# Opening the second block in one stage: norms and turning of both inputs, taps and both stores together

## The reference, cut to what matters

```python
mod_x = adaln(c, ada_w[i], ada_b[i])
mod_c = adaln(c_ctx[None], ada_w[i], ada_b[i])
h_c = modulate(ctx, norm1_g[i], mod_c[0], mod_c[1])     # rms norm, gain, scale and shift
h_x = modulate(x, norm1_g[i], mod_x[0], mod_x[1])
qkv_c, z_c, al_c, be_c, cq_c, ckv_c, kr_c, gt_c = jnp.split(h_c @ w_in[i], IN_OFFSETS, axis=-1)
qkv_x, z_x, al_x, be_x, cq_x, ckv_x, kr_x, gt_x = jnp.split(h_x @ w_in[i], IN_OFFSETS, axis=-1)
# qkv then goes through a depthwise convolution of 5 taps (conv_w) and SiLU
...
x_mid = x + mod_x[2] * mix_x                            # x itself is needed again much later
```

## Time and profile before

| | us |
|---|---|
| median of 3 runs | 3594.99 |
| lowest, highest | 3583.04, 3594.99 |
| profiled execution, its time | 3596.75 |
| profiled execution, its span | 3595.0 |
| TensorE busy (matmul) | 3052.2 (85%) |
| VectorE, ScalarE, GpSimd busy | 1256.0, 644.9, 250.3 |
| mean granted TensorE clock | 0.915 |

### The profile page before, as it was taken

The page is one execution under the profiler, slowest core; times in us unless marked ns, Lnnn a source line. Parts: engine busy times, 40 slices in busy tenths (PEclk is TensorE's granted clock), DMA queues, the critical chain, the costliest instruction groups (busy, mean ns, idle before and its releaser), DMA issues. The chain is left out here.

```text
span 3595.0 us, 44471 instructions
## 1 busy us (share of the span) xinstructions
PE 3052.2 (85%) x18941; PEld 1813.9 (50%) x18941; DVE 1256.0 (35%) x2385; ACT 644.9 (18%) x1413; POOL 250.3 (7%) x347
## 2 busy tenths in 40 slices
PE   5899398899896689997999978897977678888888
PEld 2343374346574355556888863365433343333343
DVE  1001753176343159714556545642001221111111
ACT  2000331101332135302112111431010100000000
POOL 0000010000000000003334310100000000000000
PEclk8999579898897889998999989999988879999999
DMA  9321001322001311100000012102112339999998
GB/s 313 134 70 68 0 1 38 87 72 72 1 1 46 140 36 47 34 19 9 2 2 3 2 51 87 41 1 94 70 70 82 145 134 413 413 413 413 413 413 352
DMA packets 161245, 431.74 MB, mean 120 GB/s; under 512 B 33006, under 2 KB 44530, under 8 KB 159893
## 3 DMA queue, kind: packets, MB, share of 16 engines
q1 hardware_dynamic: 161050, 428.90, 31.7%
HBM read 418.22 MB, written 10.66 MB: 119 GB/s over the span
## 5 line engine op out<-in xcount | busy, mean ns | idle before, releaser
L306 PE MATMUL banks<-weight_ring,rows_turned 128*128 128x512 f32 (+1 forms) x680 | 282.1, 575 | 33.6 <-DMA weight_ring<-in_w_in 29.5
L242 PE MATMUL banks<-weight_ring,branch_turned 128*128 128x512 f32 x640 | 280.9, 600 | 33.2 <-DMA weight_ring<-in_w_in 18.5
L2091 PE MATMUL banks<-rows_turned,weight_ring 128*128 128x256 f32 (+1 forms) x768 | 252.9, 489 | 0.8 <-PEq L431 0.5
L3140 PE MATMUL banks<-expert_weights_early,chosen_turned 128*64 128x512 f32 (+1 forms) x864 | 210.5, 563 | 20.1 <-DMA expert_weights_early<-in_w_up 15.4
L242 PE MATMUL banks<-weight_ring,rows_turned 128*128 128x512 f32 x512 | 221.6, 593 | 3.0 <-PE banks L242 1.9
L306 PEld LDWEIGHTS banks<-weight_ring,rows_turned 128*128 128x128 f32 x680 | 127.0, 197 | 186.9 <-issue 185.5
L242 PEld LDWEIGHTS banks<-weight_ring,branch_turned 128*128 128x128 f32 x640 | 122.2, 192 | 189.4 <-issue 170.7
L2091 PEld LDWEIGHTS banks<-rows_turned,weight_ring 128*128 128x128 f32 x768 | 147.2, 192 | 99.8 <-issue 84.9
L3140 PE MATMUL banks<-weight_ring,chosen_turned 128*64 128x512 f32 (+1 forms) x672 | 173.2, 570 | 13.1 <-DMA weight_ring<-in_w_up 10.5
L242 PEld LDWEIGHTS banks<-weight_ring,rows_turned 128*128 128x128 f32 x512 | 96.6, 190 | 128.0 <-issue 128.0
L242 PE MATMUL banks<-weight_ring,mix_turned 128*128 128x512 f32 x320 | 140.7, 601 | 8.4 <-DMA weight_ring<-in_l_w_out 7.1
(11 more groups left out here) (544 smaller groups left out, 4485.7 us busy)
## 6 DMA issues: line engine op xcount, KB each, us to landing
expert_weights_early<-in_w_gate SPq DMA_DIRECT2D x36, 1408.0 KB, 19.4
expert_weights_early<-in_w_up SPq DMA_DIRECT2D x36, 1408.0 KB, 16.8
expert_weights_early<-in_w_down SPq DMA_DIRECT2D x44, 1024.0 KB, 18.5
weight_ring<-in_w_gate SPq DMA_DIRECT2D x28, 1408.0 KB, 19.7
weight_ring<-in_w_up SPq DMA_DIRECT2D x28, 1408.0 KB, 17.9
weight_ring<-in_w_down SPq DMA_DIRECT2D x36, 1024.0 KB, 17.6
weight_ring<-in_l_w_in SPq DMA_DIRECT2D x15, 2048.0 KB, 8.5
weight_ring<-in_w_in SPq DMA_DIRECT2D x13, 2048.0 KB, 9.0
```

Source lines behind the costliest of these rows:

```text
L242: ins = nc.tensor.matmul(kit.ps[0:m, u % 8, 0:cols], lhsT, rhs, start=(k0 + j == 0), stop=(k0 + j == matrix.nk - 1))
L306: ins = kit.nc.tensor.matmul(kit.ps[0:m, u % self.banks, 0:cols], lhsT, rhs, start=(k == 0), stop=(k == nk - 1))
L2091: ins = nc.tensor.matmul(kit.ps[:, bank(u), 0:n], w[:, k, f * P:(f + 1) * P], hT[:, k, h0:h0 + n], start=(k == 0), stop=(k == KD - 1))
L3140: ins = nc.tensor.matmul(kit.ps[64 * s:64 * s + 64, 3 * mat + i, 0:nn], xe[:, p % 2, k0 + j, s * CAP:(s + 1) * CAP], w[s][:, j, n0:n0 + nn ...
```

## The change

The opening of the second block becomes one stage, `second_opening`, ahead of `project_and_convolve`:

- SP issues, one behind the other, the loads of the norm-1 gain, the context, the taps and the constants, then the store of x; it waits until all four tiles of x have been taken, issues the store of `h_park`, and waits for taps and constants. Both stores are waited for only in the projection's stage, behind its weight loads.
- The context has a place of its own: with the squares, the scaled rows (three rooms in place of two) and the taps it lies in `qk`, a tensor that is only written from the projection on.
- ScalarE squares x's four tiles, takes their root, takes row 0's group out of PSUM, squares the context's two tiles (waiting for their load), takes their root, and takes the groups of rows 1 to 5.
- VectorE waits for the gain first and joins it with the modulation; the rest is the order of before, over six tiles, with a second reciprocal ahead of tile 4.
- TensorE turns six tiles, then the taps (waiting for taps and constants); VectorE and ScalarE copy the taps after their last rows.
- The norm-2 gain isn't loaded here any more.

```diff
-        load(kit, [(const[:, :], a["constants2"]), (g12[:, 0, :], as_columns(a["norm1_g_2"][0])), (g12[:, 1, :], as_columns(a["norm2_g_2"][0]))])
...
-                norm_and_turn(kit, x, list(range(TX)), hT[:, :, CTX:], gx[:, 0, :], cols[:, 0:8, 0])
-                store(kit, [(x_park, x[:, :, :]), (h_park, hT[:, :, CTX:])])
-                load(kit, [(x[:, 0:TC, :], a["ctx_2"][0].rearrange("(t p) d -> p t d", p=P))])
-                norm_and_turn(kit, x, list(range(TC)), hT[:, :, 0:CTX], gx[:, 1, :], cols[:, 0:8, 1])
...
+                cwT = kit.sb(hs, "conv_w_turned", [P, 3 * HEADS, 5])
+                parked = second_opening(kit, stream, a, x, const, hT, cwT, gx, g12, cols, qk, (x_park, h_park))
+                project_and_convolve(kit, stream, m["in_first"], hT, qk, raw_v, small, cwT, parked)
...
+def second_opening(kit, stream, a, x, const, hT, cwT, gx, g12, cols, scratch, parks):
...
+        def sync(sp):
+            with nc.allow_non_contiguous_dma("columns of small vectors"):
+                sp.dma_start(g12[:, 0, :], as_columns(a["norm1_g_2"][0])).then_inc(gain_landed.sem, 16)
+                sp.dma_start(ctx[:, :, :], a["ctx_2"][0].rearrange("(t p) d -> p t d", p=P)).then_inc(ctx_landed.sem, 16)
+                sp.dma_start(cw, a["conv_w_2"][0]).then_inc(loaded.sem, 16)
+                sp.dma_start(const[:, :], a["constants2"]).then_inc(loaded.sem, 16)
+            sp.dma_start(x_park, x[:, :, :]).then_inc(parked.sem, 16)
+            for side in range(2):
+                sp.wait_ge(taken[side].sem, taken[side](TX))
+            sp.dma_start(h_park, hT[:, :, CTX:]).then_inc(parked.sem, 16)
+            sp.wait_ge(loaded.sem, loaded(32))
...
+        def scalar(act):
+            def square(i):
+                if i:
+                    act.wait_ge(sums.sem, sums(i))
+                if i == TX:
+                    act.wait_ge(ctx_landed.sem, ctx_landed(16))
+                nc.scalar.activation(sq, rows[i][0], ACT.Square, scale=D ** -0.5, accum_out=ss[:, i:i + 1]).then_inc(sums.sem, 1)
+            for i in range(TX):
+                square(i)
+            act.wait_ge(sums.sem, sums(TX))
+            root(kit, ss[:, 0:TX]).then_inc(rooted.sem, 1)
+            take(act, 1, 0)
+            for i in range(TX, R):
+                square(i)
+            act.wait_ge(sums.sem, sums(R))
+            root(kit, ss[:, TX:]).then_inc(rooted.sem, 1)
+            for i in range(1, R):
+                take(act, 1, i)
+            for g in range(1, NT // 4, 2):
+                take_taps(act, 1, g)
+
+        def vector(dve):
+            dve.wait_ge(gain_landed.sem, gain_landed(16))
+            for i in range(2):
+                ins = nc.vector.scalar_tensor_tensor(gx[:, i, :], cols[:, 8:16, i], 1.0, g12[:, 0, :], ALU.add, ALU.mult)
+            ins.then_inc(gains_ready.sem, 1)
+
+            def scale(i):
+                if i in (0, TX):
+                    end = TX if i == 0 else R
+                    dve.wait_ge(rooted.sem, rooted(1 + (i > 0)))
+                    step(dve, nc.vector.reciprocal(ss[:, i:end], ss[:, i:end]))
+                if i >= 3:
+                    dve.wait_ge(turned.sem, turned(2 * (i - 2)))
+                nc.vector.tensor_scalar(xs[:, i % 3, :], rows[i][0], ss[:, i:i + 1], None, ALU.mult).then_inc(scaled.sem, 1)
+            scale(0)
+            for i in range(R):
+                if i + 1 < R:
+                    scale(i + 1)
+                take(dve, 0, i)
+            for g in range(0, NT // 4, 2):
+                take_taps(dve, 0, g)
+
+        def tensor(pe):
...
+            for i in range(R):
+                pe.wait_ge(scaled.sem, scaled(i + 1))
...
+            pe.wait_ge(loaded.sem, loaded(32))
+            for i in range(NT // 4):
+                g = 2 * R + i
+                free(g)
+                for n in range(4):
+                    ins = nc.tensor.transpose(kit.ps[:, g % 8, 5 * n:5 * n + 5], cw[:, (4 * i + n) * P:(4 * i + n + 1) * P], kit.ident[0:5, 0:5])
+                ins.then_inc(turned.sem, 1)
...
-        load(kit, [(cw, a["conv_w_2"][0])])
-        turn(kit, [([cw[:, f * P:(f + 1) * P] for f in range(f0, f0 + 4)], cwT[:, f0:f0 + 4, :]) for f0 in range(0, NT, 4)])
...
         def sync(sp):
             stream.load_ahead(sp, matrix.last + 1, 0)
+            sp.wait_ge(parked.sem, parked(32))
```

More of the change, by code:

```diff
@@ L2004, in second_block @@
                 hT = kit.sb(hs, "rows_turned", [P, KD, CTX + SEQ])
-                norm_and_turn(kit, x, list(range(TX)), hT[:, :, CTX:], gx[:, 0, :], cols[:, 0:8, 0])
-                store(kit, [(x_park, x[:, :, :]), (h_park, hT[:, :, CTX:])])
-                load(kit, [(x[:, 0:TC, :], a["ctx_2"][0].rearrange("(t p) d -> p t d", p=P))])
-                norm_and_turn(kit, x, list(range(TC)), hT[:, :, 0:CTX], gx[:, 1, :], cols[:, 0:8, 1])
-                project_and_convolve(kit, stream, m["in_first"], a, hT, qk, raw_v, small)
+                cwT = kit.sb(hs, "conv_w_turned", [P, 3 * HEADS, 5])
+                parked = second_opening(kit, stream, a, x, const, hT, cwT, gx, g12, cols, qk, (x_park, h_park))
+                project_and_convolve(kit, stream, m["in_first"], hT, qk, raw_v, small, cwT, parked)
                 elementwise(kit, vector=lambda dve: step(dve, nc.vector.tensor_copy(ab[:, :, :], small[:, :, 0:32])))
@@ L2022, in second_block, with take, take_taps, free @@
         second_half(kit, stream, m, a, x, out, place3, (x_park, h_park, s_park, y_park, rows_park), cols)
-def project_and_convolve(kit, stream, matrix, a, hT, qk, raw_v, small):
+def second_opening(kit, stream, a, x, const, hT, cwT, gx, g12, cols, scratch, parks):
+    nc = kit.nc
+    step = kit.dve_step
+    R = TX + TC
+    NT = 3 * HEADS
+    flat = scratch[:, :, :].rearrange("p c n -> p (c n)")
+    ctx = flat[:, 0:TC * D].rearrange("p (t d) -> p t d", d=D)
+    sq = flat[:, TC * D:(TC + 1) * D]
+    xs = flat[:, (TC + 1) * D:(TC + 4) * D].rearrange("p (i d) -> p i d", d=D)
+    cw = flat[0:5, (TC + 4) * D:(TC + 4) * D + DN_QKV]
+    x_park, h_park = parks
+    parked = kit.counter("parked", 32)
+    with ExitStack() as st:
+        ss = kit.sb(st, "square_sums", [P, R])
+        rows = [(x[:, t, :], CTX + t * P, gx[:, 0, :], cols[:, 0:8, 0]) for t in range(TX)]
+        rows += [(ctx[:, t, :], t * P, gx[:, 1, :], cols[:, 0:8, 1]) for t in range(TC)]
+        gain_landed = kit.counter("gain_landed", 16)
+        ctx_landed = kit.counter("rows_landed", 16)
+        loaded = kit.counter("loaded", 32)
+        sums = kit.counter("row_sums", R)
+        rooted = kit.counter("roots_ready", 2)
+        scaled = kit.counter("rows_scaled", R)
+        turned = kit.counter("turned", 2 * R + NT // 4)
+        taken = [kit.counter("taken_dve", R + NT // 8), kit.counter("taken_act", R + NT // 8)]
+        gains_ready = kit.counter("weights_ready", 1)
+        def sync(sp):
[9 more added lines that the diff above has]
+            sp.wait_ge(loaded.sem, loaded(32))
+        def take(eng, act, i):
+            _, at, gain, shift = rows[i]
+            eng.wait_ge(turned.sem, turned(2 * i + (2 if act else 1)))
+            if i == 0:
+                eng.wait_ge(gains_ready.sem, gains_ready(1))
+            for q in range(4):
+                k = 4 * act + q
+                ps, out = kit.ps[:, (2 * i + act) % 8, q * P:(q + 1) * P], hT[:, k, at:at + P]
+                if act:
+                    ins = nc.scalar.activation(out, ps, ACT.Identity, scale=gain[:, k:k + 1], bias=shift[:, k:k + 1])
+                else:
+                    ins = nc.vector.tensor_scalar(out, ps, gain[:, k:k + 1], shift[:, k:k + 1], ALU.mult, ALU.add)
+            ins.then_inc(taken[act].sem, 1)
+        def take_taps(eng, act, g):
+            eng.wait_ge(turned.sem, turned(2 * R + g + 1))
+            src = kit.ps[:, (2 * R + g) % 8, 0:20].rearrange("w (n p) -> w n p", p=5)
+            dst = cwT[:, 4 * g:4 * g + 4, :]
+            ins = nc.scalar.activation(dst, src, ACT.Copy) if act else nc.vector.tensor_copy(dst, src)
+            ins.then_inc(taken[act].sem, 1)
+        def scalar(act):
[39 more added lines that the diff above has]
+        def tensor(pe):
+            def free(g):
+                if g >= 8:
+                    pe.wait_ge(taken[g % 2].sem, taken[g % 2]((g - 8) // 2 + 1))
+            for i in range(R):
+                pe.wait_ge(scaled.sem, scaled(i + 1))
+                for h in range(2):
+                    g = 2 * i + h
+                    free(g)
+                    for q in range(4):
+                        k = 4 * h + q
+                        ins = nc.tensor.transpose(kit.ps[:, g % 8, q * P:(q + 1) * P], xs[:, i % 3, k * P:(k + 1) * P], kit.ident[:, :])
+                    ins.then_inc(turned.sem, 1)
+            pe.wait_ge(loaded.sem, loaded(32))
+            for i in range(NT // 4):
+                g = 2 * R + i
+                free(g)
+                for n in range(4):
```

(9 more changed lines are left out.)

## The result

The changed kernel takes 3552.9 us (median of 4 runs, 3550.57 to 3559.5) against 3590.74 for the one before (4 runs, 3583.04 to 3594.99): 37.8 us less, ratio 0.990 with a 95% interval of 0.9876 to 0.9924. Timed again in five rounds, it was 3549.96 against 3591.51, ratio 0.9886 (0.9868 to 0.9905). Both intervals exclude no change. The forecast was 3557, or 38 us less than the 3594.99 that it started from; with a fourth run the median of before is 4.25 lower.

The account below looks back on a forecast made before the run. TensorE idles in the second block's opening, a 61.0 us relay of loads, norms and stores. One stage saves 36.6 us, or 39.1 with a warm clock; 38 taken from 3594.99 gives 3557 us, range 3543 to 3572 (eight in ten).

Parts of the forecast that it names:

- Start: Opening: ScalarE's squares no longer wait for a load, first square at 1219.05, roots ready at about 1225.4.
- Gain: Opening: VectorE waits for the norm gain behind 2 MB of weights, released at 1227.2, reciprocal at 1227.65.
- ScalarE's chain: Opening: longest chain after the reciprocal, ScalarE's takes, context squares, root and tap copies, about 15.2 us to the stage's end.
- Context, stores, constants: Opening's transfers: hidden under compute; context's load costs nothing up to 5.5 us, stores nothing up to 6.1.
- series rival: Opening, row 4: its scaling waits for the context's root, so both norms run in series; 3560 us, chance 0.07.
- stores' rival: Projection's start: h_park's 6.1 us beside the first products slows TensorE or shows as a wait; -32, 3563 us, chance 0.05.
- Opening in sum: Addition's end to first product: projection starts at 1243.2 in place of 1279.77, 36.6 us earlier.
- Clock: Projection's first unit: starts at 2.4 GHz instead of 1.2, worth 2.5 us, at about six in ten.
- rival 2: Cold start: clock back at 1.2 GHz when the projection begins; -36.6 or a little less, 3558.5 us, chance 0.25.
- warm start: Projection: first unit in 3.4 us at 2.4 GHz instead of 5.9, worth 2.5 us.
- The rest: Later stages: same lengths, but for a few microseconds of clock either way; wrong if over 8 us.

Follow-up runs that it names:

- experiment 2: Changed kernel with the gain's load issued last, behind context, taps, constants and x_park: opening 33.45 us, profiled once, not timed.
- experiment 4: Changed kernel with the projection's third weight group issued behind x_park instead of ahead of the gain: opening 21.83 us, first unit 6.51.
- experiment 1: Changed kernel with one wait more, for both stores inside the opening's stage: opening 27.13 us, 4.6 longer; first unit 5.62.
- experiment 6: Experiment 4's kernel with context squares early, taps turned between rows, and four filler products behind TensorE's last transposes: opening 20.01 us, first unit 3.73.
- experiment 7: Changed kernel with filler products behind rows 3 and 4 and behind the taps: opening 23.87 us, first unit 4.06.
- experiment 9: Changed kernel unedited and experiment 6's kernel, each reprofiled and timed in five rounds: 3549.96 and 3548.29 us, against 3591.51 for before.
- x7: The kernel of experiment 6, with fillers; timed at 3548.29 us, ratio to before 0.9887.
- x8: The kernel of experiment 7, the changed kernel with fillers: opening 23.87 us, first unit 4.06.
- a2: Second profile of x7, unedited, in experiment 9: opening 21.70 us, first unit 3.73; timed at 3548.29 us.
- experiment 3: Changed kernel with the old order of norms in one stage, context loaded after both stores: 3571.24 us against 3592.6 for before, ratio 0.9938.

## Why the prediction was right, step by step

**Start.** ScalarE's first square stood 0.29 us after the addition's end, as forecast, and the roots were ready at 1223.96, 6.6 after it.

**Gain.** Forecast: the reciprocal 8.9 us after the addition. Measured: 7.90. The gain landed behind the weights, as the second layer's did, but released VectorE 8.35 us after the weights' issue and not 9.07 as the earlier trace rows say. The two gain instructions took 0.16 from the first's start to the reciprocal's, not 0.37: they no longer wait for each other. Experiments 2 and 4 show from both sides that place in the queue sets this landing (7.74 us behind one weight load, 18.68 behind 6 MB, 2.45 behind nothing).

**ScalarE's chain.** Forecast 15.2 us from reciprocal to the stage's end, measured 14.3 (1225.26 to 1239.56). The first take ended and the first square of the context began without the gap that I had left; five takes took 7.08 instead of 7.35; and the taps' last copy ended 0.24 behind the last take instead of 0.6. ScalarE ended last, as forecast; VectorE's last take ended at 1238.02.

**Context, stores, constants.** Free, as forecast. The series rival is refuted by ScalarE's rows: the context's root ran at 1232.04, while TensorE was still turning row 3. The margin at the root was thin: it ended at 1232.33 and VectorE came for it at 1232.59. TensorE's idle 0.99 us before row 4 is VectorE's pace. The stores' rival is refuted by the first unit: with h_park beside it, it takes no longer than its time at the low clock explains (experiment 1), and 3.73 us in experiment 6.

**Opening in sum.** Forecast 24.5 us, that is 36.6 saved; measured 22.5 and 38.5. Both terms that were too large were too large by about 1 us.

**Clock.** The step that failed. I took a projection starting at 2.4 GHz at six in ten, worth 2.5 us; the first unit took 6.39 us, as rival 2 had it, and 0.46 more than before. In every opening traced here the clock rose while TensorE did nothing but transposes: in the changed kernel at 1231.6, 5.3 us after the first of them. The Trainium skill's rule that transposes don't count for the clock (TensorE: Matmul & The Clock Gate, Part 4: PE-mode transpose) is not what this shows. These transposes are of float32, though, and no trace here shows whether they run in the mode that the page means. The clock then fell as the last small transposes ended. What exactly lets it fall I could not settle: filling the gaps didn't hold it (experiment 7), and ending with large products held it in one profile and not in another of the same kernel (experiments 6 and 9).

That the forecast of 38 us saved was nearer than its parts is luck: the opening gave 38.5 instead of 36.6, and the clock took 0.5 instead of giving 1.4. The relay turned into one stage was right; the warm start was not, and two errors of opposite sign cancelled.

**The rest.** I had allowed a few microseconds of clock in later stages, of either sign. In the first profile they were 6.7 us in favour. The first of their two parts moves from run to run (delta net with its surroundings 523.7 and 526.8 us in two profiles of the changed kernel). The second does not: from the second load of h_park to the router, 386.1 and 386.2 us in both profiles of before, 382.8 in both of the changed kernel. It isn't a lasting property of the new opening either, for x7, x8 and a2, which have it too, show 385.9, 386.0 and 386.1. The traces show where the two kinds part. In the kernels of 386 us SP takes 5.5 to 5.8 us to issue that stretch's first three weight loads, and the first product comes 17.3 to 17.8 us after the load of h_park; in those of 382.8 it is 4.4 to 4.6 us and 15.9 to 16.2. Later 32 transposes start 148.1 to 148.4 us into the stretch instead of 147.4 to 147.9, and take 6.4 to 6.6 us instead of 5.0 to 5.3, as the clock rises at 154.1 instead of 150.6. Why SP takes longer in some kernels stays open. So what the traces show is 38.0 us from the opening and 3.4 us from a stage that the change doesn't contain, beside medians that fell by 37.8 and 41.5.

## What to carry to other kernels

A relay of small load, norm, store, load, norm is worth one stage: what was 61 us here became 22.5. By experiment 3, some 14.5 of the 38.5 us came from small loads put beside arithmetic, 4.6 from issuing the first store early, and 18.0 from no longer waiting for the second store and the next input's load before the second norm. Inside such a stage, sort SP's issues by who waits for them first, since here a transfer of 4 KB landed behind all that was issued ahead of it (experiment 2); the bulk that nobody needs soon, weights included, goes last. Once the transfers are hidden, a few microseconds won in one place are easily lost in another. Of the 3.3 to 5.2 us won in the traces by further reordering and fillers, 3.1 to 3.2 were given back in a stretch of identical instructions over a millisecond later, and 1.7 were left in the medians, which can't be told from none. So the whole trace has to be compared, from the change to the end.

## What the runs showed of the hardware that was not expected

- One stage of identical instructions took 294.2 to 313.9 us for its 1578 products over twelve traces, at mean granted clocks of 0.86 to 0.79; in the two traces of the changed kernel alone it was 301.3 and 311.5.
- Another kept one of two lengths by kernel, 382.7 to 382.9 us or 385.9 to 386.2, the same in both traces of each of the three kernels that were profiled twice. All three traces with fillers, and both of the kernel before, had the longer one.
- TensorE's granted clock can fall while the engine is all but continuously busy (at 1239.3 in experiment 7, at 1222.9 within row 5's transposes in the second profile of experiment 9).
- The gain's 4 KB in elements of 4 bytes took 2.2 us from issue to VectorE's release when it stood first in SP's order (1213.78 to 1215.96, experiment 4).
